# Two transformer blocks on one core: weights ahead of tables, small copies between units, and sums, groups and last units in another order

## The chip, the core and the metric

The kernel runs on one core of a Trainium2 chip. A core has five engines that run side by side: TensorE (PE in the profile) multiplies matrices into PSUM, VectorE (DVE) and ScalarE (ACT) work elementwise, GpSimd (POOL) does so too but reads and writes SBUF only here, and SyncE (SP) issues transfers. Sixteen DMA engines move data between HBM and SBUF. Engines meet through semaphores only, and each works through its own instructions strictly in order. The metric is the time of one execution on the device in microseconds (us); smaller is better.

## What is computed

Two transformer blocks, one after the other, on 256 tokens of 1024 columns, all in float32. The first block has two layers: a mixer of three attentions, a cross-attention to a memory of 256 tokens, and a gated feed-forward (FFN). The second block takes a context of 256 tokens as well. Its shifts, scales and gates come from two vectors times a large matrix `ada_w` (adaLN).

```python
for l in range(DEPTH):                                   # first block, DEPTH = 2
    h = rmsnorm(x, g_mix_pre[l])
    ... = jnp.split(h @ w_in[l], IN_SPLITS, axis=-1)     # three attentions on the parts
    x = x + rmsnorm(concatenate([o_a, o_b, o_c]) @ w_out[l], g_mix_post[l])
    xo = cross_attention(rmsnorm(x, g_x_pre[l]), rmsnorm(mem, g_x_mem[l]), w_xq[l], w_xkv[l], w_xo[l])
    x = x + rmsnorm(xo, g_x_post[l])
    gate, up = jnp.split(rmsnorm(x, g_ffn_pre[l]) @ w_ffn_in[l], 2, axis=-1)
    x = x + rmsnorm((jax.nn.silu(gate) * up) @ w_ffn_out[l], g_ffn_post[l])
for i in range(DEPTH):                                   # second block
    m = (s_c @ ada_w[i] + ada_b[i]); mc = (s_cc @ ada_w[i] + ada_b[i])
    x = half_step_ffn(x, m[:, 0], m[:, 1], m[:, 2], ffn_w_in[i, 0], ffn_w_out[i, 0], ...)
    ...                                                  # context too (i = 0), then
    ...                                                  # neighbourhood attention (i = 0) or convolution (i = 1)
    x = half_step_ffn(x, m[:, 6], m[:, 7], m[:, 8], ffn_w_in[i, 1], ffn_w_out[i, 1], ...)
```

## The kernel before

**The stream of weights.** All weights are laid out as 654 units of up to 128 x 1024 numbers, and every unit goes the same way. SP loads it into `land`, a ring of four slots. ACT rounds it into `w_hi` (`split`, L892). POOL writes the rest, `land` minus `w_hi`, into `w_lo` in two halves (`lo`, L787). PE multiplies twice 2 tiles of tokens with it, three products for each (hi by hi, lo by hi, hi by lo: L2138 to L2140), so a unit costs PE 12 matmuls. SP may load unit u once POOL has done unit u-4 (semaphore `lo_ready`), ACT may split it once PE has done u-4 (`w_used`), and PE waits for `lo_ready` of the unit itself. The first four units' `w_lo` are made by DVE.

**By unit or by tile.** `group` takes four units one after the other with both token tiles (12 matmuls to a unit). `group_by_tile` takes the four units for token tile 0 (6 matmuls each), then again for tile 1; only the second pass gives the units free. `first_group` uses the latter. Its `aside` form, in the FFN that takes x into the second block and in the first product of the neighbourhood attention (`products`, weights `na_w_kv`), puts its results in the PSUM banks `TURN` and `OUT` so that it need not wait for banks 0 to 3, in which the norm before it is still worked on.

**The opening.** `make_h(now=True)` turns x into h: PE transposes it, DVE scales it, ACT writes `h_hi` (`high`), DVE `h_lo`. In this ACT also splits units 0 to 3 and, in `load_constants`, issues nine transfers: eight tables (semaphore `start_in`) and the memory (`io`). In `products_in` (weights `w_in`, groups g = 0 to 3 of four units, so units 0 to 15) ACT's `tables` squares the memory, waits for the eight tables and for DVE's angles (`start_v`), and computes exponentials, cosines and sines. After it stand the next splits. `turn_mem` transposes the memory after group 1. `kv_weights` follows: seven copies of `na_rpb`, each of 1024 rows of 64 numbers from HBM to HBM (`rpb_w`), then the 16 units of `w_xkv`, used in `mixer_prep` and in the mixer's attention.

**The adaLN sums.** `ada_w` comes in 36 groups of four pieces, loaded by SP between the units (`ada_begin`, `ada_finish`), each piece once DVE has done with the same piece of the group before. DVE multiplies and adds a group (`ada_sums`, L2048 and L2051; 16 steps in groups 0 to 9, where both vectors count, 8 later), PE adds over partitions (`ada_sum`, L2739 and L2740), and DVE adds the bias (`ada_rows_out`, L2071). Only then may the next group be summed. Where the sums stand is written by hand: one in each turn of an `ffn_in` loop, one in `products_q`, one or two in `products_y` for `w_xo`, and some in `ffn_out` after the units named in `ADA_OUTS`.

**The end of an FFN.** `ffn_out` has 22 units; k counts them. The last four go to token tile 0 first, its left half of columns over the four units, then its right half, each half ending with `y_ready`. Tile 1 follows. Where `then` is given, PE transposes the next input before the last four (`make_h`), and `turn_free` there waits for the last sum to be out (`ada_sum`).

**Before the neighbourhood attention** SP has `load_tables` asked: after four units of the next weights it loads a mask, a table and 24 quarters of biases (`load_bias`, L723), and then the next unit.

## Time and profile before

| | us |
|---|---|
| median of 3 runs (2251.19 to 2258.12) | 2252.46 |
| the profiled execution, by the same clock | 2254.71 |
| its span from the first to the last instruction | 2252.8 |
| PE busy (matmul) | 2154.2, 96% of the span |
| POOL busy | 1686.8, 75% |
| ACT busy | 1070.5, 48% |
| DVE busy | 966.1, 43% |

All later times are microseconds from the span's start. A row of the timeline gives an instruction's start and length, and in brackets how long its engine was idle before it and who released it. Busy time of PE is modelled for pipelined matmuls, so it is read for gaps, not for peak rate. [...]

### The profile page before, as it was taken

Reading aid. Unit: us, or ns where it says so; the run is one execution under the profiler, and the core shown is the slowest. Engines: PE = TensorE matmul, PEld = TensorE weight load, DVE = VectorE, ACT = ScalarE, POOL = GpSimd, SP = SyncE. Lnnn points to the kernel's source line nnn. Section 1 sums busy time; section 2 is a strip of 40 time slices with the busy share of each in tenths; the row PEclk is TensorE's granted clock in tenths of the full one; section 3 lists DMA queues with packets and bytes.
Section 4 is the critical chain, followed back from the end, with each engine's and each line's share of the span. In section 5 each row is a group of like instructions: output and inputs, shape, how many; then the busy total and the mean of one; then the engine's idle time right before and its main releaser. Section 6 shows DMA issues by size and latency. Waiting matters only on the chain.

```text
span 2252.8 us, 32261 instructions
## 1 busy us (share of the span) xinstructions
PE 2154.2 (96%) x10197; PEld 1741.4 (77%) x10197; DVE 966.1 (43%) x1892; ACT 1070.5 (48%) x1646; POOL 1686.8 (75%) x1361
## 2 busy tenths in 40 slices
PE   8998899999988999999999999999999999999997
PEld 6787778778877787788778877887887788687886
DVE  6355676753556544544543552364111310344112
ACT  4464444445653544444454454565444544435442
POOL 5646388877544888798888879726988888697986
PEclk9999999999999999999999999999999999999999
DMA  7535387755244786687878765523656566464663
GB/s 232 165 113 163 103 296 257 261 182 166 92 138 179 260 284 255 211 300 244 296 255 284 282 218 162 187 76 113 203 179 198 166 186 207 139 222 145 193 205 120
DMA packets 135863, 447.10 MB, mean 198 GB/s; under 512 B 22539, under 2 KB 28131, under 8 KB 135769
## 3 DMA queue, kind: packets, MB, share of 16 engines
q1 hardware_dynamic: 129080, 426.62, 57.4%
q10 hardware_dynamic: 6688, 19.23, 2.5%
q8 instruction: 58, 0.95, 0.2%
q14 instruction: 37, 0.30, 0.0%
HBM read 444.60 MB, written 3.03 MB: 199 GB/s over the span
## 4 chain that ended last, share of the span: by engine, by line
POOL 49%; issue 29%; PE 20%; DVE 1%; POOLq 1%; ACT 0%; DMA 0%; SPq 0%; ACTq 0%; DVEq 0%
POOL w_lo L787 48%; PE ps L2138 5%; PE ps L2140 5%; PE ps L2139 5%; PE ps L2647 1%; PE ps L2612 1%; PE ps L2635 1%; PE ps L2475 1%; POOLq L187 0%; PE ps L2608 0%; POOL ada_land L833 0%; POOLq L785 0%; PE ps L2578 0%; PE ps L2390 0%; PE ps L2580 0%
## 5 line engine op out<-in xcount | busy, mean ns | idle before, releaser
L787 POOL TENSOR_TENSOR w_lo<-land,w_hi 128x512 fp32r<-128x512 f32 x1300 | 1650.3, 1303 | 518.0 <-ACT w_hi L892 516.9
L892 ACT ACTIVATE w_hi<-land 128x1024 fp32r<-128x1024 f32 x654 | 692.5, 1061 | 942.4 <-PE ps L2140 736.9
L2138 PE MATMUL ps<-w_hi,h_hi 128*128 128x512 f32 (+1 forms) x1840 | 734.6, 399 | 52.8 <-POOL w_lo L787 24.4
L2140 PE MATMUL ps<-w_hi,h_lo 128*128 128x512 f32 (+1 forms) x1840 | 720.6, 392 | 0.0
L2139 PE MATMUL ps<-w_lo,h_hi 128*128 128x512 f32 (+1 forms) x1840 | 719.5, 391 | 0.0
L2138 PEld LDWEIGHTS ps<-w_hi,h_hi 128*128 128x128 f32 x1840 | 348.0, 189 | 150.1 <-POOL w_lo L787 39.6
L2140 PEld LDWEIGHTS ps<-w_hi,h_lo 128*128 128x128 f32 x1840 | 347.8, 189 | 74.0
L2139 PEld LDWEIGHTS ps<-w_lo,h_hi 128*128 128x128 f32 x1840 | 348.4, 189 | 67.3
L1530 DVE TENSOR_TENSOR hid_lo<-ps,hid_hi 128x512 f32 (+1 forms) x77 | 53.2, 691 | 550.5 <-ACT hid_hi L1044 550.5
L2138 PE MATMUL ps<-w_hi,hid_hi 128*128 128x512 f32 x616 | 245.2, 398 | 5.7 <-POOL w_lo L787 5.7
L2140 PE MATMUL ps<-w_hi,hid_lo 128*128 128x512 f32 x616 | 243.5, 395 | 0.0
L2139 PE MATMUL ps<-w_lo,hid_hi 128*128 128x512 f32 x616 | 243.4, 395 | 0.0
L2051 DVE SCALAR_TENSOR_TENSOR ps<-ada_land,ccol,ps 128x512 f32<-128x512 f32 x322 | 230.5, 750 | 20.6 <-DMA ada_land<-ada_w_dram 12.6
L2138 PEld LDWEIGHTS ps<-w_hi,hid_hi 128*128 128x128 f32 x616 | 115.7, 188 | 36.5 <-POOL w_lo L787 7.9
L2140 PEld LDWEIGHTS ps<-w_hi,hid_lo 128*128 128x128 f32 x616 | 115.7, 188 | 28.0
L2139 PEld LDWEIGHTS ps<-w_lo,hid_hi 128*128 128x128 f32 x616 | 115.8, 188 | 27.0
L1128 ACT ACTIVATE h_hi<-ps 128x512 fp32r<-128x512 f32 x56 | 33.0, 597 | 61.6 <-DVE ps L1479 33.1
L2138 PE MATMUL ps<-w_hi,m_hi 128*128 128x512 f32 x128 | 53.6, 418 | 5.1 <-POOL w_lo L787 3.6
L1647 DVE TENSOR_TENSOR hid<-ps,sg 128x256 f32<-128x256 f32 x110 | 41.1, 415 | 37.8 <-ACT sg L1038 37.8
L1727 DVE SCALAR_TENSOR_TENSOR ps<-ps,rows 128x512 f32<-128x512 f32 x24 | 15.9, 693 | 93.2 <-PE ps L2140 93.2
L2140 PE MATMUL ps<-w_hi,m_lo 128*128 128x512 f32 x128 | 51.2, 400 | 0.0
L2139 PE MATMUL ps<-w_lo,m_hi 128*128 128x512 f32 x128 | 51.2, 400 | 0.0
(276 smaller groups left out, 1911.4 us busy)
## 6 DMA issues: line engine op xcount, KB each, us to landing
land<-ffn_w_in_dram SPq DMA_DIRECT2D x220, 512.0 KB, 3.6
ada_land<-ada_w_dram SPq DMA_DIRECT2D x144, 512.0 KB, 5.2
land<-ffn_w_out_dram SPq DMA_DIRECT2D x110, 512.0 KB, 4.1
land<-w_ffn_in_dram SPq DMA_DIRECT2D x88, 512.0 KB, 3.9
land<-w_ffn_out_dram SPq DMA_DIRECT2D x44, 512.0 KB, 4.1
land<-na_w_qkv_dram SPq DMA_DIRECT2D x40, 512.0 KB, 4.2
land<-w_xkv_dram SPq DMA_DIRECT2D x32, 512.0 KB, 3.6
land<-w_in_dram SPq DMA_DIRECT2D x32, 488.0 KB, 3.5
```

The costliest lines, as they stand in the source:

```text
L787: done = pool.tensor_tensor(w_lo[:, slot, half], land[:, slot, half], w_hi[:, slot, half].bitcast(F32), ALU.subtract)
L892: act.activation(w_hi[:, slot, :], land[:, slot, :], ACT.Copy).then_inc(*my.up("hi_ready"))
L1128: act.activation(half_of(h_hi, i), turned_bank(i), ACT.Copy).then_inc(*my.up("split_hi"))
L1530: dve.tensor_tensor(lo_dst, bank(TURN + kp).rearrange("p (a b) -> p a b", a=2), hi_src.bitcast(F32), ALU.subtract).then_inc(*my.up("split_ ...
L1647: ins_ = dve.tensor_tensor(hid[:, g % 2, t, :], got, sg[:, t, :], ALU.mult)
L2051: ins_ = dve.scalar_tensor_tensor(acc, w, c, acc, ALU.mult, ALU.add)
L2138: pe.matmul(dst, lh, wh, start=first, stop=False)
L2139: pe.matmul(dst, lh, wl, start=False, stop=False)
L2140: done = pe.matmul(dst, ll, wh, start=False, stop=last)
L2475: done = pe.transpose(ps[0:m, b, c * SEQ + t * P:c * SEQ + (t + 1) * P], tile, ident[:, :])
L2612: yield pe.matmul(s[:, t * SEQ:(t + 1) * SEQ], q[:, t * P:(t + 1) * P], k, start=(c == 0), stop=(c == len(mp["qk"]) - 1))
L2635: done = pe.transpose(ps[:, TURN + m % 2, at * P:(at + 1) * P], e[:, j * P:(j + 1) * P], ident[:, :])
```

## The change

Five things, none of which changes what is computed.

1. **Opening.** The eight small tables are issued by SP, after unit 3, and not by ACT. ACT writes the first piece of `h_hi` ahead of its first split, and issues only the memory, after the last piece of `h_hi`. `tables` is cut in two: the squares of the memory come after the split of unit 7, the rest after that of unit 8 (both came after unit 6).
2. **Small copies.** The seven copies of `na_rpb` are issued one by one behind units 7 to 13 of the 16 of `w_xkv`, no longer ahead of them.
3. **adaLN sums.** In `products_q` the first result is moved out between the two halves of the sum's steps. In `products_y` PE's sum stands after the fourth unit's first pass, not the third; where two groups are loaded, the second starts at unit 5, not 3, and its last pieces all follow unit 7. In `ffn_out` the sums move from units 7, 12, 17 to 8, 13, 17 (layer 0 of the first block), from 7, 13 to 8, 13 (layer 1), and from 7, 12, 17 to 8, 12, 16 (the two FFN halves that open the second block); SP starts loading each three units ahead, not two.
4. **First group aside.** It goes unit by unit.
5. **Last four units.** Tile 0 takes both halves of units 0 and 1, then the left half of 2 and 3, then their right halves.

```diff
-ADA_OUTS, ADA_OUTS_2, COLUMNS_AT = (7, 12, 17), (7, 13), 9
+ADA_OUTS, ADA_OUTS_2, ADA_OUTS_3, COLUMNS_AT = (8, 13, 17), (8, 13), (8, 12, 16), 9
...
+LAST_FOUR = ((0, 0), (0, 1), (1, 0), (1, 1), (2, 0), (3, 0), (2, 1), (3, 1))
...
+            def products_in(l):
+                stream(f"w_in{l}", 0, 16, None if l else {RING - 1: load_constants})
...
             def kv_weights(w):
                 if n_kv[0] == 0:
-                    for j in range(7):
...
-                stream(w, 0, KV_UNITS)
+                    stream(w, 0, KV_UNITS, {RPB_AT + j: lambda j=j: shifted_rpb(j) for j in range(7)}, rolled=False)
+                else:
+                    stream(w, 0, KV_UNITS)
...
-                extra = ada_extra([3] if keys else [0, 3][0:sums])
+                extra = ada_extra([3] if keys else [0, 5][0:sums])
+                if sums > 1:
+                    late = [extra.pop(at) for at in (8, 9)]
+                    extra[7] = lambda steps=[extra[7], *late]: [step() for step in steps]
...
-                extra = ada_extra([at - 2 for at in ada])
+                extra = ada_extra([at - 3 for at in ada])
...
                 if l == 0:
+                    split(RING)
+                    square_memory()
+                    split(1)
+                    tables()
                     split(RING - 1)
-                    tables()
-                    split(RING + 1)
...
                 if now:
+                    high(0)
                     split(1)
-                    high(0)
                     high(1)
                     split(RING - 1)
-                    load_constants()
                     high(2)
                     high(3)
+                    load_io("mem")
                     return
...
             def products_q(w):
                 dve.wait_ge(*my.last())
-                ada_sums()
+                ada_steps(range(0, KC // 2))
                 scaled_out("q_x", 0, GW, 0, R_X, "taken")
-                dve.wait_ge(*my.last())
+                ada_sums(range(KC // 2, KC))
                 ada_rows_out()
...
             def first_group(width, aside):
 
-                group_by_tile((TURN, OUT) if aside else (0, 2), width, fresh=True, aside=aside)
-                if aside:
+                if not aside:
+                    group_by_tile((0, 2), width, fresh=True)
+                else:
+                    pe.wait_ge(sems["split_lo"], my.at("split_lo", n["split_lo"]))
+                    group((TURN, OUT), width)
...
                 if sums:
-                    after[2] = ada_sum
+                    after[3] = ada_sum
...
-                for half in range(2):
-                    for j in range(4):
-                        if half == 0:
-                            pe.wait_ge(sems["lo_ready"], my.at("lo_ready", u + j + 1))
-                        done = part(u + j, FC - 4 + j, {0: (half,)})
-                    done.then_inc(*my.up("y_ready"))
+                for j, half in LAST_FOUR:
+                    if half == 0:
+                        pe.wait_ge(sems["lo_ready"], my.at("lo_ready", u + j + 1))
+                    done = part(u + j, FC - 4 + j, {0: (half,)})
+                    if j == 3:
+                        done.then_inc(*my.up("y_ready"))
```

In what order the instructions now stand is shown at three places. ACT at the opening, before: the end of `load_constants`, the last two pieces of `h_hi`, the squares of x, three splits, then all of `tables`.

```order
L909 DMA ghead<-diff_head_g_dram 128x128
L909 DMA io<-mem_dram 128x2x1024
L1128 ACTIVATE h_hi<-ps 128x4x128 x2
L1095 ACTIVATE z,stat<-x 128x1024 x2
L1079 DMA rows<-g_mix_post_dram 128x1024
L1082 DMA vals<-mla_w_q_up_dram 128x2x384
L1083 DMA vals<-mla_w_kv_up_dram 128x512
L892 ACTIVATE w_hi<-land 128x1024 x3
L927 ACTIVATE z,stat<-io 128x1024 x2
L929 ACTIVATE csig<-ccol 128x16
L931 ACTIVATE lam<-lam 128x4
L932 ACT_TABLE_LOAD
```

The same stretch of ACT in the changed kernel, from the splits of units 1 to 3 on.

```order
L920 ACTIVATE w_hi<-land 128x1024 x3
L1144 ACTIVATE h_hi<-ps 128x4x128 x2
L1102 DMA io<-mem_dram 128x2x1024
L1111 ACTIVATE z,stat<-x 128x1024 x2
L1095 DMA rows<-g_mix_post_dram 128x1024
L1098 DMA vals<-mla_w_q_up_dram 128x2x384
L1099 DMA vals<-mla_w_kv_up_dram 128x512
L920 ACTIVATE w_hi<-land 128x1024 x4
L939 ACTIVATE z,stat<-io 128x1024 x2
L920 ACTIVATE w_hi<-land 128x1024
L943 ACTIVATE csig<-ccol 128x16
L945 ACTIVATE lam<-lam 128x4
```

The two pieces of `h_hi` no longer stand behind transfers, and two more splits stand ahead of the exponentials. DVE in `products_q` (layer 0), before: 16 steps of a sum (L2048, L2051), its rounding, and then the first result (`tok_x`).

```order
L2048 TENSOR_SCALAR ps<-ada_land,ccol 128x512 x2
L2051 SCALAR_TENSOR_TENSOR ps<-ada_land,ccol,ps 128x512 x14
L2057 CAST ada_hi<-ps 128x512 x2
L2060 TENSOR_TENSOR ada_lo<-ps,ada_hi 128x512 x2
L1556 TENSOR_SCALAR tok_x<-ps,stat 128x512 x2
L2071 TENSOR_TENSOR ada_o<-ps,ada_b 2x512
```

And in the changed kernel:

```order
L2063 TENSOR_SCALAR ps<-ada_land,ccol 128x512 x2
L2066 SCALAR_TENSOR_TENSOR ps<-ada_land,ccol,ps 128x512 x6
L1572 TENSOR_SCALAR tok_x<-ps,stat 128x512 x2
L2066 SCALAR_TENSOR_TENSOR ps<-ada_land,ccol,ps 128x512 x8
L2078 CAST ada_hi<-ps 128x512 x2
L2081 TENSOR_TENSOR ada_lo<-ps,ada_hi 128x512 x2
L2092 TENSOR_TENSOR ada_o<-ps,ada_b 2x512
```

The first result went ahead of half the steps and of the rounding. SP at `products_y` of `w_xo` in layer 1, before, from the third unit on: the piece of `ada_land` that belongs to the second group stands, with the one before it (x2), ahead of the fifth unit.

```order
L621 DMA land<-w_xo_dram 128x1024
L576 DMA ada_land<-ada_w_dram 128x1024
L621 DMA land<-w_xo_dram 128x1024
L576 DMA ada_land<-ada_w_dram 128x1024 x2
L621 DMA land<-w_xo_dram 128x1024
L589 DMA ada_m<-ada_o 2x512
L594 DMA ada_b<-ada_b_dram 1x512
L576 DMA ada_land<-ada_w_dram 128x1024
L621 DMA land<-w_xo_dram 128x1024
```

And in the changed kernel:

```order
L625 DMA land<-w_xo_dram 128x1024
L580 DMA ada_land<-ada_w_dram 128x1024
L625 DMA land<-w_xo_dram 128x1024
L580 DMA ada_land<-ada_w_dram 128x1024
L625 DMA land<-w_xo_dram 128x1024
L593 DMA ada_m<-ada_o 2x512
L598 DMA ada_b<-ada_b_dram 1x512
L625 DMA land<-w_xo_dram 128x1024
L580 DMA ada_land<-ada_w_dram 128x1024
L625 DMA land<-w_xo_dram 128x1024
```

The fifth and sixth units now stand ahead of every piece of the second group.

## Rows read from the trace of the kernel before

**Rows 1.** Page: busy (share) xinstructions; POOL's `w_lo` (xcount, busy, mean ns, idle, releaser)

```profile
PE 2154.2 (96%) x10197; PEld 1741.4 (77%) x10197; DVE 966.1 (43%) x1892; ACT 1070.5 (48%) x1646; POOL 1686.8 (75%) x1361
...
L787 POOL TENSOR_TENSOR w_lo<-land,w_hi 128x512 fp32r<-128x512 f32 x1300 | 1650.3, 1303 | 518.0 <-ACT w_hi L892 516.9
```

**Rows 2.** PE's waits over the span: us in total, times, longest

```profile
PE ps L2138 <- POOL w_lo L787: 33.7, 37, 4.6
```

**Rows 3.** Stretches: length; busy (x) of PE, PEld, DVE, ACT, POOL; PEclk, DMA, GB/s

```profile
37.00:44.00 7.00, 6.01 (x17) 5.00 (x18) 6.79 (x8) 1.87 (x3) 6.95 (x6) 0.52 0.49 143
...
71.00:75.00 4.00, 4.00 (x11) 3.13 (x12) 3.62 (x18) 2.54 (x4) 4.00 (x4) 0.57 0.53 153
225.00:232.00 7.00, 4.83 (x16) 4.20 (x17) 2.12 (x4) 1.46 (x3) 3.61 (x3) 0.51 0.53 214
...
45.20:66.74 21.54, 21.54 (x99) 18.13 (x98) 9.05 (x25) 6.92 (x12) 13.91 (x11) 1.00 0.90 232
```

**Rows 4.** Timeline of ACT in the opening: start, us, what, [idle before, releaser]

```profile
18.18 0.60 ACT L1128 ACTIVATE h_hi<-ps 128x512 fp32r<-128x512 f32 x1 [5.29 <-issue]
...
27.58 1.06 ACT L927 ACTIVATE z<-io 128x1024 f32<-128x1024 f32 x1 [2.55 <-DMA io<-mem_dram]
...
32.55 0.20 ACT L931 ACTIVATE lam<-lam 128x4 f32<-128x4 f32 x1 [2.67 <-DVE lam L1437]
...
34.32 3.88 ACT L892 ACTIVATE w_hi<-land 128x1024 fp32r<-128x1024 f32 x4
```

**Rows 5.** Timeline of PE in the opening: units 0, 7 and 16

```profile
19.65 0.46 PE L2138 MATMUL ps<-w_hi,h_hi 128*128 128x488 f32 x1 [0.61 <-DVE h_lo L1488]
...
37.99 0.78 PE L2138 MATMUL ps<-w_hi,h_hi 128*128 128x488 f32 x1 [4.65 <-POOL w_lo L787]
...
70.94 0.50 PE L2138 MATMUL ps<-w_hi,m_hi 128*128 128x512 f32 x1 [3.60 <-POOL w_lo L787]
```

**Rows 6.** Timeline of SP's queue: the seven small copies

```profile
49.67 7.87 SPq L671 DMA_DIRECT2D rpb_w<-na_rpb_dram  x7
```

**Rows 7.** Timeline of PE and DVE in `products_q`, layer 0

```profile
227.17 1.97 PE L2475 MATMUL ps<-ident,tok_x 128*128 128x128 f32 x8 [4.93 <-DVE tok_x L1556]
...
213.85 9.31 DVE L2051 SCALAR_TENSOR_TENSOR ps<-ada_land,ccol,ps 128x512 f32<-128x512 f32 x14
```

**Rows 8.** Timeline of SP, DVE and PE at `w_xo`, layer 1

```profile
681.25 30.48 SPq L576 DMA_DIRECT2D ada_land<-ada_w_dram  x2
...
726.65 0.69 DVE L2060 TENSOR_TENSOR ada_lo<-ps,ada_hi 128x512 fp32r<-128x512 f32 x1
...
729.24 0.50 PE L2138 MATMUL ps<-w_hi,h_hi 128*128 128x512 f32 x1 [0.41 <-POOL w_lo L787]
```

**Rows 9.** Timeline of PE and DVE at `w_xo`, layer 0

```profile
270.38 0.39 PE L2739 MATMUL ps<-ada_hi,pick_r 128*2 128x512 f32 x1 [2.52 <-DVE ada_lo L2060]
...
276.53 1.28 DVE L1698 SCALAR_TENSOR_TENSOR x<-ps,stat,x 128x1024 f32<-128x1024 f32 x1
```

**Rows 10.** Timeline of PE at sums inside `ffn_out`: layer 0, layer 1, second block

```profile
437.09 0.40 PE L2739 MATMUL ps<-ada_hi,pick_r 128*2 128x512 f32 x1 [1.22 <-DVE ada_lo L2060]
...
892.55 0.39 PE L2739 MATMUL ps<-ada_hi,pick_r 128*2 128x512 f32 x1 [1.08 <-DVE ada_lo L2060]
...
1118.21 1.94 PE L2506 MATMUL ps<-ident,x 128*128 128x128 f32 x16 [1.07 <-DVE ada_o L2071]
```

**Rows 11.** Timeline of PE and ACT at the first group aside, in `ffn_in`

```profile
1133.98 0.50 PE L2138 MATMUL ps<-w_hi,h_hi 128*128 128x512 f32 x1 [1.24 <-POOL w_lo L787]
...
1138.95 1.21 ACT L1209 ACTIVATE z<-ps,stat 128x1024 f32<-128x1024 f32 x1
```

**Rows 12.** Timeline of SP and PE at the first group aside, weights `na_w_kv`

```profile
1319.20 15.88 SPq L723 DMA_DIRECT2D ada_land<-rpb_w  x24
...
1343.40 0.47 PE L2138 MATMUL ps<-w_hi,h_hi 128*128 128x512 f32 x1 [0.28 <-POOL w_lo L787]
```

**Rows 13.** Timeline of PE in the last FFN: the last of its 22 units

```profile
2232.09 0.50 PE L2138 MATMUL ps<-w_hi,hid_hi 128*128 128x512 f32 x1 [1.69 <-POOL w_lo L787]
```

61 lines of the change are left out of this document (33 added, 28 removed).

## The prediction

> **What bounds the kernel now.** I read the page first, then the list of waits, then the timeline of each place that the diff touches. PE is busy for 96% of the span. POOL, next in line, works 2 x 1.303 = 2.61 us on a unit of weights and still idles 518 us waiting for ACT, whose splits wait for PE to free the ring [rows 1]. PE itself takes 2.69 us for a unit: 8 units in the 21.54 us of a stretch without any wait [rows 3]. So PE is the bound, by a margin of 3% over POOL, and a time is gained only where PE stands still or runs at its lower clock, and only if no other chain is next in line there. Standing still for POOL's `w_lo` sums up to 33.7 us in 37 waits [rows 2]. After a long stop the granted clock is at about half: 0.52 in 37 to 44, 0.57 in 71 to 75, 0.51 in 225 to 232 [rows 3]; each follows a stop of 3.6 to 4.9 us [rows 5, 7]. A removed stop therefore gives back more than its own length.
>
> **The opening.** Three things go. (a) ACT writes the third piece of `h_hi` after 5.29 us in which it only issued transfers, and PE then waits 0.61 us for `h_lo` [rows 4, 5]; now the pieces are ready first. With the first piece ahead of the first split DVE starts about 0.4 us sooner. I take 1.0 together. (b) ACT splits unit 7 at 34.32, behind `tables`: it waited 2.55 us for the memory and 2.67 us for DVE's angles, and PE stood 4.65 us [rows 4, 5]. The splits of units 7 and 8 now stand ahead. (c) That stop was followed by the lower clock. PE ended unit 7 at 43.0, 5.0 us after its start instead of 2.7: 2.3 us.
> What is late next? POOL needs the split of unit 8 at about 31. ACT has unit 7 split at about 25, the squares take 2.1 us, so the memory may land as late as 28; it is issued some 3 us earlier than before, when it had landed by 27.58 [rows 4]. DVE can start the angles at about 21, after the norm of x, instead of 25, so they end near 28, the memory's norm at 30.5 and the first result at 32; PE wants that at 34.4. The distances (6 us before, beside POOL) and the second result end near 44, and PE wants them at 47. All hold with 2 to 3 us to spare. PE's path then is its own pace.
> (d) The seven copies took SP 7.87 us to issue, ahead of unit 16, and PE stood 3.60 us for that unit [rows 6, 5]; the unit itself then took 4.3 us at half clock instead of 2.7 [rows 3]. Together 5.2. The copies' new place costs nothing: one is 1.1 us of issue, and behind it a unit of weights is asked for about three units ahead of its use, 8 us at PE's full pace and more in the mixer's attention. If this cover were gone, a unit would be late by a copy's stay on the DMA engines.
> Sum of the opening: 1.0 + 4.65 + 2.3 + 5.2 = 13.2 us.
>
> [...] The rows say that the eight tables cost ACT its issue time, 5.29 us, of which PE saw 0.61 [rows 4, 5]. [...]
>
> **The sum in `products_q`, layer 0.** PE stands 4.93 us for `tok_x`, which DVE writes only after 16 steps (14 of them take 9.31) and the rounding [rows 7]. Now 8 steps, 5.3 us, stand ahead of it, so it is out at 219.3 and PE, there at 222.2, does not stop. The lower clock after the stop cost 2.1 us more (8 transposes and 12 matmuls). In exchange the sum is ready only at 227.1 (8 steps 5.3, rounding 2.6), where PE arrives at 225.9: a new wait of 1.2. Net 5.8. Layer 1 has sums of 8 steps and no such stop: 0.
>
> **The sums at `w_xo`.** In layer 0 PE waits 2.52 us for DVE [rows 9]; one pass of a unit later, 1.4 us less. But behind it PE needs the new x, which DVE ends at 277.8 [rows 9] at the end of a chain that starts from the same sum. Of 1.4 only 0.2 arrive. In layer 1 SP held the fifth unit behind a piece of the second group for 30 us [rows 8], and PE ran through five waits, the last at 729.24. Now two more units are there early, and the second group is DVE's: it ends at 727.34 [rows 8], PE's second pass can begin at 728.3 instead of 730.6, and DVE's chain to x gives back 1.4 of these 2.3. Take 1.4.
>
> **The sums in `ffn_out`.** Layer 1: the wait of 1.08 goes, with what its first matmul shows around it 1.2. Second block, both halves: the wait of 1.07 for `ada_o` [rows 10] is covered by one more unit: 1.2 for the first; the second is dealt with below. Layer 0 is different: a sum there takes DVE 15.1 us (437.09 [rows 10] to the next at 452.2), and 13 to 17 are four units, 11.2 us. The first wait of 1.22 goes, but the third sum comes 3 x 15.1 us after DVE's start plus the 1.4 us that DVE now waits for PE at unit 8. PE stands 2.7 us at unit 17 and passes it 1.3 us later than before. The 0.63 us wait in its last four units goes with that. Net a loss of 0.5.
>
> **The first group aside.** By tile, PE takes 1.35 us for a unit that POOL needs 2.6 for, so the first pass has waits of 1.24, 0.82 and 0.81 (the first is in [rows 11]); by unit it has none. In `ffn_in` ACT cannot split the next unit before it has normalised, at 1138.95 + 1.21 [rows 11], so PE, done sooner, waits for it: of 3.9 us I keep 2.2. Before the neighbourhood attention nothing is kept. There the next unit is not asked for before SP has issued 24 biases, 15.88 us, until 1335.1; it reaches PE at 1343.40 [rows 12]. The waits removed (the sum's 1.2, the passes' 2.9) come back as one stop of about 6 us before that same unit. Stops of 3.6 to 4.9 us were followed by half clock three times out of three [rows 3]. One unit then takes 5 us instead of 2.7, two can be hit; and DVE copies x beside POOL earlier. Bounds: -4.5 and +0.5 (nothing lost, the ring fuller). I take -2.5.
>
> [...]
>
> **The last four units.** The last of the 22 units is ready 1.69 us after PE wants it [rows 13], in three FFNs (also at 1732.77 and 1931.51). Now PE has two more parts of 0.70 us to do first: 1.4 each. In the last FFN DVE's chain starts at the end of the first left half, which the same `w_lo` sets, and is busy from there to the end: only 0.5. First `y_ready` comes 1.4 us later against the second, which hides a scaling of 0.7. Sum 3.3.
>
> **Total.** 13.2 + 5.8 + 0.2 + 1.4 + 1.2 + 1.2 - 0.5 + 2.2 - 2.5 + 3.3 = 25.5 us. Against the profiled execution, 2254.7 with a span of 2252.8, this gives 2229.2; the median of the runs lies 2.2 lower, 2252.5, so I forecast 2227.0.
>
> **Rivals.**
> - *Half clock stays away before the neighbourhood attention, and chains give more back.* For it: 2 us stops are often not followed by the lower clock. Then -2.5 becomes 0, and layer 0 or `w_xo` may give 2 more: 2222.5.
> - *The opening is held by another chain.* DVE's distances run beside POOL, and if they or the memory end 3 to 5 us later than I count, PE stops again and half clock follows (2 us): 7 us lost, 2234.
> - *The gain stays off the path, POOL being the bound.* The chain of waits goes through POOL for half of the span, and POOL's pace is only 3% under PE's. Then only stops in which POOL idled too are worth something, the opening's 13.2 and little else: 2239. Against it: POOL's 518 idle us end with ACT, whose waits end with PE [rows 1].
> - *Slower: the small copies starve the mixer.* The seven copies lie between units 7 and 14 on SP's queue. If each holds the unit behind it past PE's need, by its stay on the DMA engines (7 copies and a unit kept the DMA full for some 11 us, 1.6 each), and PE comes back at half clock each time (2.3), that is 7 x 3.9 = 27 us and cancels the rest: 2254; with stops of over 1.8 us the kernel is slower. It decides when a unit is asked for less than 5 us ahead; it is asked for over 8.
> - *The change does not do what it says*: ACT would have to reach `tables` before unit 7 all the same. The order shown rules it out.
>
> **Chances.** Forecast 0.60, better case 0.16, opening held 0.14, POOL as bound 0.06, copies 0.03, the rest 0.01. The forecast's own bounds are 2222 to 2232, from the -4.5 to +0.5 and some 2 us for where the clock's changes fall. With the rivals on both sides but the last ones: 2219 to 2237. About 0.3% (6.8 us) is what a measurement of this kernel can tell from no change: faster 0.95, same 0.03, slower 0.02.
>
> **What would show it.** Right: no wait over 1 us of PE for `w_lo` before 60 us, the first matmul of unit 16 near 58; no stop for `tok_x`, and a wait of about 1.2 for `ada_lo` behind it; a stop of 2 to 3 us for `ada_lo` at unit 17 of layer 0's `ffn_out`; a stop of 5 to 6 us for `w_lo` near 1310 with a clock near 0.5 behind it; 0.3 instead of 1.69 at the last units. Wrong: PE waiting for `zin` or the memory in the opening, ACT waiting for `w_xkv` to land in the mixer, or PE's busy time at full clock growing.

## The result, and the profile after

The kernel after takes 2226.45 us (median of 4 runs, 2223.64 to 2231.67), the kernel before 2255.29 beside it (4 runs, 2251.19 to 2261.65). The ratio is 0.987, 95% interval 0.984 to 0.991. The forecast was 2227.0, with bounds of its own from 2222 to 2232, and 2219 to 2237 with the rivals on both sides, so the time came out as forecast. The profiled execution of after took 2223.64 us, 5.4 and 8.0 less than the upper two of the four runs: that gap is the part of the story the forecast did not have.

The page of after answers [rows 1]: PE is busy 13.1 us less, with the same 10197 multiplications, and POOL idles 29 us less.

```profile
PE 2141.1 (96%) x10197; PEld 1735.5 (78%) x10197; DVE 968.2 (44%) x1892; ACT 1069.0 (48%) x1646; POOL 1684.8 (76%) x1361
...
L815 POOL TENSOR_TENSOR w_lo<-land,w_hi 128x512 fp32r<-128x512 f32 x1300 | 1648.4, 1300 | 489.4 <-ACT w_hi L920 488.0
```

PE's list of waits over the span (us in total, times, longest) answers [rows 2]. Waits for `w_lo` fell from 33.7 us in 37 to 18.6 in 22, but the longest grew from 4.6 to 7.4; waits for the adaLN sums, 6.1 us in 4 before, stand in the second row.

```profile
PE ps L2159 <- POOL w_lo L815: 18.6, 22, 7.4
PE ps L2763 <- DVE ada_lo L2081: 9.1, 5, 2.8
```

Both kernels issue PE's multiplications in nearly the same order, so the n-th of before can be set against the n-th of after. The difference of their starts, in the two profiled executions, grows where after gains. Each row below is read between two places at which it stands still; the last row takes the difference of the two spans. PEclk is TensorE's granted clock as a share of full speed. Half clock is a stretch in which it read 0.50, as from 38 to 44 us of before; a figure between 0.50 and 1.00 is the mean of a stretch with both.

| place | difference at the end of it, us | gained there | forecast |
|---|---|---|---|
| opening: units 0 to 3 | 1.9 | 1.9 | 1.0 |
| opening: units 7 and 8 | 9.5 | 7.6 | 6.95 |
| opening: unit 16 | 14.9 | 5.4 | 5.2 |
| `products_q`, layer 0 | 20.7 | 5.8 | 5.8 |
| `w_xo`, layer 0 | 21.65 | 1.0 | 0.2 |
| sums in `ffn_out`, layer 0 | 21.1 | -0.5 | -0.5 |
| half clock that only before had (484, 624 us), and cross-attention of layer 1 | 23.05 | 1.9 | none |
| `w_xo`, layer 1 | 24.8 | 1.7 | 1.4 |
| sums in `ffn_out`, layer 1 | 26.0 | 1.2 | 1.2 |
| second block, first half | 27.2 | 1.3 | 1.2 |
| first group aside, `ffn_in` | 29.6 | 2.3 | 2.2 |
| before the neighbourhood attention | 27.6 | -2.0 | -2.5 |
| last four units | 31.0 | 3.4 | 3.3 |

The timeline of PE in after at the places of [rows 5, 7, 10, 12, 13] (start, length, what, in brackets the idle time before and its releaser). Unit 7 and unit 16 follow the work ahead of them without a stop: they have no bracket.

```profile
31.35 0.38 PE L2159 MATMUL ps<-w_hi,h_hi 128*128 128x488 f32 x1
...
57.60 0.48 PE L2159 MATMUL ps<-w_hi,m_hi 128*128 128x512 f32 x1
...
212.31 0.40 PE L2763 MATMUL ps<-ada_hi,pick_r 128*2 128x512 f32 x1 [1.30 <-DVE ada_lo L2081]
...
447.06 0.40 PE L2763 MATMUL ps<-ada_hi,pick_r 128*2 128x512 f32 x1 [2.81 <-DVE ada_lo L2081]
...
1316.19 0.77 PE L2159 MATMUL ps<-w_hi,h_hi 128*128 128x512 f32 x1 [7.42 <-POOL w_lo L815]
...
2201.72 0.50 PE L2159 MATMUL ps<-w_hi,hid_hi 128*128 128x512 f32 x1 [0.34 <-POOL w_lo L815]
```

The third row is the small wait that `products_q` was to get in exchange (forecast 1.2, read 1.30), the fourth the one at unit 17 of layer 0's `ffn_out` (forecast 2.7, read 2.81), the fifth the long stop (forecast about 6, read 7.42), the last the remainder at the last units (forecast 0.3, read 0.34). The stretches around the old and the new stop (length; busy time of PE, PEld, DVE, ACT, POOL; PEclk; DMA; GB/s) answer [rows 3]: full clock where before had half, and half where the new long stop is.

```profile
37.00:44.00 7.00, 7.00 (x33) 5.94 (x32) 6.86 (x7) 4.27 (x9) 6.96 (x6) 1.00 0.67 210
1312.00:1319.00 7.00, 2.81 (x7) 2.26 (x8) 4.11 (x3) 3.66 (x4) 6.44 (x5) 0.53 0.60 209
```

### The profile page after: what moved, and what is told of

The parts are those of the page before. It is cut to its first block, busy times and chain, and to the rows that moved or that the text cites. A ratio compares the mean times of both kernels' runs of the same rounds, so it can differ in the third digit from the quotient of the medians.

```text
span 2221.8 us, 32201 instructions
## 1 busy us (share of the span) xinstructions
PE 2141.1 (96%) x10197; PEld 1735.5 (78%) x10197; DVE 968.2 (44%) x1892; ACT 1069.0 (48%) x1646; POOL 1684.8 (76%) x1361
## 4 chain that ended last, share of the span: by engine, by line
POOL 49%; issue 27%; PE 21%; DVE 2%; POOLq 1%; DMA 0%; ACT 0%; SPq 0%; ACTq 0%; DVEq 0%
POOL w_lo L815 48%; PE ps L2159 6%; PE ps L2161 6%; PE ps L2160 6%; PE ps L2671 1%; PE ps L2636 1%; PE ps L2659 1%; PE ps L2499 1%; POOLq L191 0%; PE ps L2632 0%; POOL ada_land L861 0%; POOLq L813 0%; PE ps L2602 0%; PE ps L2414 0%; DMA cols<-cols_dram 0%
```

## The experiments

Every kernel below is the kernel after with the edit shown. The difference of starts is now taken against after's profiled execution, at the place of the edit, since whole runs of one kernel lie up to 0.4% apart.

### The order of ACT's splits

```diff
                 if l == 0:
-                    split(RING)
+                    split(RING - 1)
                     square_memory()
-                    split(1)
                     tables()
-                    split(RING - 1)
+                    split(RING + 1)
```

> The kernel after, but ACT does the squares of the memory and all of tables behind the split of unit 6 again, as before; the eight tables stay on SP's queue. If the order of ACT's splits is what took the stop of unit 7 away (the prediction's step b), a stop comes back there, of the length that the later of two ends dictates: the memory lands in time now, DVE's angles end at 28.6, the sines at 30.5, the split of unit 7 at 31.5, and PE wants the unit at 31.35: a stop of 1 to 2 us, without half clock, 14.9 us of gain by unit 16 become 13 to 14. If the earlier landing had nothing to do with it (only order counts), the whole stop of about 5 us and its half clock return: the gain is about 8. If the order counts for nothing, no stop and no loss.

One run took 2229.70 us. PE in it, at unit 7:

```profile
34.03 0.49 PE L2158 MATMUL ps<-w_hi,h_hi 128*128 128x488 f32 x1 [2.63 <-POOL w_lo L815]
```

The stop is back with 2.8 us lost and no half clock behind it. So both halves count: the order takes 2.8 us away. The rest of the 7.6 us that were gained at units 7 and 8 remains in this kernel, in which ACT began the squares of the memory at 23.49 with no wait, where [rows 4] had 27.58. That the earlier issue of the tables and the memory gives this rest is got by subtraction, not by a run of its own. The stop is longer than the 1 to 2 us that I expected, because I counted to the end of the split: POOL's two halves, 2.6 us, stand between it and PE.

### Who issues the tables

```diff
-                stream(f"w_in{l}", 0, 16, None if l else {RING - 1: load_constants})
+                stream(f"w_in{l}", 0, 16, None)
...
                     split(RING - 1)
+                    load_constants()
                     high(2)
```

> The kernel after, but ACT issues the eight tables itself, behind the split of unit 3 and ahead of the third piece of h_hi; all else stays. By the prediction's step a this is worth ACT's issue time as far as PE saw it: a wait for h_lo of 0.6 to 1 us returns and the gain by unit 16 falls from 14.9 to about 14, with no stop for unit 7 or 8. The rival, that the tables held ACT and DVE through their later landing: DVE's angles start some 5 us later, its distances and second result go past 47 us, and PE stops for these by 3 us or more between units 8 and 16: a gain of 11 or less.

One run took 2233.61 us. DVE's `h_lo`, the first of its operations on the positions, and PE's transposes of the memory in it:

```profile
16.93 1.29 DVE L1520 TENSOR_TENSOR h_lo<-ps,h_hi 128x512 fp32r<-128x512 f32 x2 [1.71 <-ACT h_hi L1159]
...
23.70 1.01 DVE L1454 CAST pos_r<-pos_i 128x256 f32<-128x256 int32 x1 [1.58 <-DMA ghead<-diff_head_g_dram]
...
38.74 3.06 PE L2526 MATMUL ps<-ident,io 128*128 128x128 f32 x16 [4.40 <-DVE zin L1588]
```

6.4 us are lost by unit 9, and the rival is the one that describes it: the tables held DVE through their landing (positions at 23.70 instead of 19.00), and DVE's first result (`zin`) held PE. The wait for `h_lo`, by which the prediction priced ACT's issue time, did not come back: `h_lo` starts at 16.93 where before had 18.82, and PE keeps level with after, within 0.2 us, up to 30 us. The 6.4 are measured against an execution of after in which PE had no stop for `zin`. Six others with after's opening had one and were 4.4 to 4.8 us later than it by unit 9 (below); against those, the tables on ACT's queue cost 1.5 to 2.0. ACT's issue time, 5.29 us in before, of which PE saw 0.61, was the wrong measure for them: the queue's issue stands ahead of the landing of the last table (`diff_head_g`, issued at 14.98 us here and at 7.80 in after), and what waits for that is a chain on another engine.

### The seven small copies

```diff
-                    stream(w, 0, KV_UNITS, {RPB_AT + j: lambda j=j: shifted_rpb(j) for j in range(7)}, rolled=False)
+                    for j in range(7):
+                        shifted_rpb(j)
+                    stream(w, 0, KV_UNITS)
```

> The kernel after, with the seven copies ahead of unit 16 again. Theory (step d): PE stops for unit 16 by about 3.6 us and works it at half clock, 5.2 us in all, and the copies' new place had cost nothing, so the gain falls by 5.2 and by nothing else. Rival: the ring is fuller at this place than it was before, so that the 7.9 us of issue are hidden in part: a loss under 2 us.

One run took 2230.24 us. SP's issue of the copies, and PE at unit 16:

```profile
41.90 8.30 SPq L691 DMA_DIRECT2D rpb_w<-na_rpb_dram  x7
...
61.87 0.50 PE L2161 MATMUL ps<-w_hi,m_hi 128*128 128x512 f32 x1 [3.73 <-POOL w_lo L817]
```

5.6 us are lost there (0.3 to 5.9 behind after), forecast 5.2. From there to 440 us the difference stays within 0.25; later it moves between 5.5 and 8.3, mostly with half clock that falls at other places in the two executions. The copies' new place cost nothing: against before, after's gain stays at 14.9 from 76 to 200 us.

### `products_q` in its old order

```diff
-                ada_steps(range(0, KC // 2))
+                ada_sums()
                 scaled_out("q_x", 0, GW, 0, R_X, "taken")
-                ada_sums(range(KC // 2, KC))
+                dve.wait_ge(*my.last())
                 ada_rows_out()
```

> The kernel after, with products_q in its old order: all steps of the sum and its rounding ahead of the first result. Theory: PE stops 4.9 us for tok_x in layer 0, half clock costs 2.1 behind it, and the wait of about 1.2 for the sum goes: a loss of 5.8, and nothing in layer 1. Rival: the loss is made good further on, at the wait for x behind w_xo, whose chain starts from a sum: then less than 3 us are left by the end of layer 0.

One run took 2240.85 us. PE, and the stretch around it with a granted clock of 0.58:

```profile
217.96 1.97 PE L2499 MATMUL ps<-ident,tok_x 128*128 128x128 f32 x8 [4.98 <-DVE tok_x L1572]
...
214.00:221.00 7.00, 3.04 (x11) 2.76 (x12) 3.87 (x6) 2.25 (x3) 5.34 (x5) 0.58 0.82 322
```

The difference goes from 5.6 to 11.1: 5.5 us, forecast 5.8. Up to the last sum of layer 0, at 447 us of after, it stays at 11.1, so nothing was made good. Most of the rest of this run's length lies in the opening (4.6) and in half clock near 1461 us (3.2), both below.

### The sums of layer 0

```diff
-ADA_OUTS, ADA_OUTS_2, ADA_OUTS_3, COLUMNS_AT = (8, 13, 17), (8, 13), (8, 12, 16), 9
+ADA_OUTS, ADA_OUTS_2, ADA_OUTS_3, COLUMNS_AT = (7, 12, 17), (8, 13), (8, 12, 16), 9
```

> The kernel after, with the sums of layer 0's ffn_out back at units 7, 12 and 17 (SP still three units ahead). The prediction put the new places there at a loss of 0.5 us, its argument being that DVE's 15.1 us for a sum don't fit between 13 and 17. Theory: by the end of this FFN 0.5 us are won, the wait at the first sum, 3.2 us in the kernel after, becoming one of 1.2 at the first and one or two smaller. Rival: the gap at 443.9 comes from DVE's late start and is there whatever the places are; no difference.

One run took 2236.84 us, and yet the place itself gains: the difference falls from 5.4 to 4.0 over the three sums, 1.4 us. The first sum waits 1.23 us, the third not at all:

```profile
420.87 0.39 PE L2763 MATMUL ps<-ada_hi,pick_r 128*2 128x512 f32 x1 [1.23 <-DVE ada_lo L2081]
```

The forecast of -0.5 for the edit holds against before (21.65 to 21.1). The undone edit gains more than that: the two things the edit did together, later places and an earlier start of SP's loading, are then worth -1.4 and, by subtraction, +0.9. `result_first` below, which has the same places, gains the same 1.4. I had expected 0.5, or nothing.

### The long stop: by tile, and with PE kept busy

```diff
...
-                first_group(width, aside)
+                if aside:
+                    group_by_tile((TURN, OUT), width, fresh=True, aside=True)
+                    for t in range(T):
+                        name, value = free[t]
+                        pe.wait_ge(sems[name], my.at(name, value))
+                else:
+                    first_group(width, aside)
                 group((1, 3), width)
```

> The kernel after, with the first group aside of the neighbourhood attention by tile again; that of ffn_in stays by unit. The prediction put this part at -2.5 us there together with a gain of 1.2 from the sum ahead of it. Theory: three waits of 0.8 to 1.2 us return, the one stop of 7.8 shrinks to 4 to 5, and half clock stays or goes by that: a gain of 0 to 2.5 us against the kernel after. Rival: the unit behind the biases comes at the same time whatever stands ahead, so nothing changes within 0.5 us.

One run took 2237.25 us. At the place, three waits are back (the first is shown) and the long one shrinks to 2.20:

```profile
1308.89 0.50 PE L2159 MATMUL ps<-w_hi,h_hi 128*128 128x512 f32 x1 [1.25 <-POOL w_lo L815]
...
1323.13 0.47 PE L2159 MATMUL ps<-w_hi,h_hi 128*128 128x512 f32 x1 [2.20 <-POOL w_lo L815]
...
1320.00:1327.00 7.00, 4.38 (x19) 3.03 (x18) 5.86 (x5) 3.89 (x5) 6.51 (x5) 1.00 0.63 221
```

The clock stays full (the last row), and the difference goes from 8.6 to 7.3: by tile was better here by 1.35 us. To part the half clock from the stop, the next kernel fills it:

```diff
                 first_group(width, aside)
+                if aside:
+                    hold(1, 8)
                 group((1, 3), width)
```

> The kernel after, with eight multiplications of no use (0.85 us each, into bank 1, which the next group overwrites) in the stop of 7.8 us before the second group of the neighbourhood attention. The stop itself stays as long, since it ends with w_lo. If the half clock of 1312 to 1319 us comes from the stop, it goes, and with it 2 to 3 us; the loss of the first group aside there falls from 8.6 (7.8 and what stands around it) to about 6. If the clock fell for another reason, it stays and nothing changes, or the held PE starts the group later, by up to 1 us.

One run took 2230.82 us. `hold` runs until 1322.46, PE then waits 0.73 more for the unit, and the stretch behind it is at full clock, where after had 0.77 in the matching one:

```profile
1315.43 7.03 PE L2167 MATMUL ps<-dist,ident 128*128 128x512 f32 x16
1323.18 0.50 PE L2159 MATMUL ps<-w_hi,h_hi 128*128 128x512 f32 x1 [0.73 <-POOL w_lo L815]
...
1323.00:1330.00 7.00, 6.82 (x30) 5.64 (x31) 0.00 (x0) 2.54 (x3) 7.00 (x7) 1.00 0.52 166
```

So the half clock comes from the stop. The other profiled executions agree: the nine of after's kind whose stop here was 4.4 us or longer had half clock at it, the three whose stop was 2.2 or less had none. It is worth 1.2 us (6.8 to 5.6), not 2 to 3: half of the 7 us at half clock lay in the stop itself, and what PE lost in the next unit it had in part from waits for POOL that were there anyway. The rest of the loss is the stop.

### The biases spread

```diff
-                stream("na_w_qkv" if w == "na_w_kv" else w, first, 4 * groups)
+                if w == "na_w_kv":
+                    stream("na_w_qkv", first, 4 * groups, {RING + 1 + 2 * h: lambda h=h: load_bias(h) for h in range(NA_BIAS - 1)} | {4 * groups - 1: lambda: load_bias(NA_BIAS - 1)}, rolled=False)
+                else:
+                    stream(w, first, 4 * groups)
...
                 sp.dma_start(ada_land[:, 1, T * SEQ:T * SEQ + 128], ins["na_rope"]).then_inc(sems["na_in"], 16)
-                for h in range(NA_BIAS):
-                    load_bias(h)
```

> The kernel after, with the 24 transfers of biases not in one piece ahead of the second group of the neighbourhood attention, but four behind every second unit of na_w_kv. Theory (the stop of 7.8 us is SP's 15.8 us of issue ahead of the next unit): the stop and the half clock go, unless DVE's or ACT's work on x is next in line: 7 to 9 us faster than the kernel after. Rival: ACT's split of the next unit waits for the norm of x as in ffn_in, so a stop of 3 to 4 us stays, without half clock: 4 to 6 us faster. Against it all: each set of four holds the unit behind it, four stops of 1 us or more: no gain.

Four runs, median 2224.35 us (2220.69 to 2227.04), ratio to before 0.987, 0.984 to 0.990. SP now issues four quarters, then two units, in turn, and PE's longest wait at the place is 1.41:

```profile
1306.63 2.54 SPq L754 DMA_DIRECT2D ada_land<-rpb_w  x4
1309.22 2.38 SPq L625 DMA_DIRECT2D land<-na_w_qkv_dram  x2
1311.64 2.37 SPq L754 DMA_DIRECT2D ada_land<-rpb_w  x4
...
1316.16 0.47 PE L2160 MATMUL ps<-w_hi,h_hi 128*128 128x512 f32 x1 [1.41 <-POOL w_lo L816]
...
1311.26 1.21 ACT L1226 ACTIVATE z<-ps,stat 128x1024 f32<-128x1024 f32 x1
1312.37 2.94 ACT L921 ACTIVATE w_hi<-land 128x1024 fp32r<-128x1024 f32 x3
```

The difference goes from 6.0 to 0.25, so 5.8 us are won at the place: the rival's 4 to 6, for its reason, though its stop of 3 to 4 us is three waits of 2.3 together. The last two rows show it: ACT writes the norm of x first and splits the next units behind it, as in `ffn_in`. 1.6 us of the gain are lost again near 1450 us, below.

### The late edits undone

```diff
-ADA_OUTS, ADA_OUTS_2, ADA_OUTS_3, COLUMNS_AT = (8, 13, 17), (8, 13), (8, 12, 16), 9
+ADA_OUTS, ADA_OUTS_2, ADA_OUTS_3, COLUMNS_AT = (8, 13, 17), (7, 13), (7, 12, 17), 9
-LAST_FOUR = ((0, 0), (0, 1), (1, 0), (1, 1), (2, 0), (3, 0), (2, 1), (3, 1))
+LAST_FOUR = ((0, 0), (1, 0), (2, 0), (3, 0), (0, 1), (1, 1), (2, 1), (3, 1))
```

> The kernel after, with three late edits undone at places that can be read apart: the sums of layer 1's ffn_out at 7 and 13, those of the second block's two opening halves at 7, 12 and 17, and the last four units by whole half columns. Theory, term by term: 1.2 us lost at the first sum of layer 1; 1.2 in the first half of the second block; in its second half the 1.2 are lost ahead of the first group aside and given back at the stop of 7.8 us; and in the last four units 1.4 lost in two FFNs and 0.5 in the last. Rival (POOL is the bound, so what PE loses here was waiting behind it anyway): each of these places loses under 0.5 us.

One run took 2231.57 us. Lost against after: 0.9 at layer 1's sums, 1.27 in the second block's first half, 1.27 in its second half ahead of the aside group, and 1.36, 1.36 and 0.6 in the three FFNs whose last unit PE waits for. That is theory's list, and the rival with POOL as the bound falls. The 0.9 is the weakest of them: kernels without this edit lost 0.2 to 1.1 at the same place against after, which has no wait there. PE in the second half, and at the stop behind it:

```profile
1292.07 1.94 PE L2530 MATMUL ps<-ident,z 128*128 128x128 f32 x16 [1.07 <-DVE ada_o L2092]
...
1320.71 0.77 PE L2159 MATMUL ps<-w_hi,h_hi 128*128 128x512 f32 x1 [4.36 <-POOL w_lo L815]
```

But the stop gives back 2.9 us, more than the 1.27. The rest points at SP's queue. Its waits in after, in the 27 us ahead of the biases, hold one that the same stretch of before does not have (the first row); with the sum back at unit 17 it is 2.7 (the second row, of `late_undo`):

```profile
SPq L593 <- DVE ada_o L2092: 3.8, 1, 3.8
...
SPq L593 <- DVE ada_o L2092: 2.7, 1, 2.7
```

SP stores a sum's result once the next sum's pieces are through. In before that store stood behind unit 19 of this FFN's 22, the edits (a sum earlier by one unit, loading a unit earlier too) put it behind unit 17, and SP stood there 3.8 us for a result that was not yet out. It reached the biases 6.6 us after PE's transposes began (1291.15 against 1284.53 on PE) where before and this kernel had 3.9 (1319.20 against 1315.33, 1295.93 against 1292.07). Of these 2.75 us, 1.25 are PE's own lead, the wait for the sum that is gone, and 1.5 are SP's delay. Without that delay the stop would have been near the forecast 6. The delay came with the sum's new place: eleven more profiled executions that have it show 0.8 to 1.9 us of it, `late_undo` none. But `late_undo` too had 2.7 us of the wait, so that the longer wait for the store makes the delay is argued, and not shown apart from the rest of the edit.

### Why the executions of after fall in two groups

Six kernels whose opening is that of after had, in their profiled execution, a stop which after's lacks. This is `bias_spread`:

```profile
37.21 2.79 PE L2511 MATMUL ps<-ident,io 128*128 128x128 f32 x16 [3.27 <-DVE zin L1573]
```

| profiled execution | DVE begins the angles (`ang`) | POOL begins | ahead by | PE's granted clock 10 to 16 us | PE waits for `zin` | PE by unit 9, later than after |
|---|---|---|---|---|---|---|
| `after` | 19.54 | 20.58 | 1.04 | 0.72 | 0 | 0 |
| `after_again` | 19.44 | 20.38 | 0.94 | 0.72 | 0 | -0.25 |
| `copies_ahead` | 19.71 | 20.87 | 1.16 | 0.72 | 0 | +0.3 |
| `clock_hold` | 19.80 | 19.99 | 0.19 | 1.00 | 3.27 | +4.5 |
| `aside_by_tile` | 20.05 | 20.25 | 0.20 | 1.00 | 3.20 | +4.7 |
| `q_undo` | 19.92 | 20.14 | 0.22 | 1.00 | 3.24 | +4.6 |
| `sums_layer0` | 19.81 | 19.98 | 0.17 | 1.00 | 3.27 | +4.4 |
| `late_undo` | 19.71 | 19.89 | 0.18 | 1.00 | 3.24 | +4.4 |
| `bias_spread` | 20.19 | 20.38 | 0.19 | 1.00 | 3.27 | +4.8 |

DVE's angles are a dozen small operations, each waiting for the last. The same one of them, first in after, then in `bias_spread`, and the start of POOL in each (rows in this order):

```profile
20.07 0.18 DVE L1443 TENSOR_SCALAR ang<-ang 128x32 f32<-128x32 f32 x1
...
21.75 1.22 DVE L1444 TENSOR_SCALAR ang<-ang 128x32 f32<-128x32 f32 x1
...
20.58 29.95 POOL L815 TENSOR_TENSOR w_lo<-land,w_hi 128x512 fp32r<-128x512 f32 x23 [19.60 <-ACT w_hi L920]
...
20.38 12.65 POOL L816 TENSOR_TENSOR w_lo<-land,w_hi 128x512 fp32r<-128x512 f32 x10 [19.40 <-ACT w_hi L921]
```

In after it took 0.18 us, before POOL had begun; in `bias_spread` 1.22, with POOL at work: about one half of a `w_lo` (1.27). Not all of DVE's small operations are slowed. Beside the same POOL, those of 128 x 2 numbers with an operand in PSUM take 0.17 (the first row, of after), and so does one of 128 x 1 in SBUF (the second). Then come the first result in `bias_spread` and in after:

```profile
29.31 0.17 DVE L1401 SCALAR_TENSOR_TENSOR ps<-ps,newton 128x2 f32<-128x2 f32 x1
...
33.34 0.15 DVE L1472 TENSOR_SCALAR lam<-lam 128x1 f32<-128x1 f32 x1
...
35.80 1.36 DVE L1573 TENSOR_SCALAR zin<-ps,stat 128x488 f32<-128x488 f32 x2
...
30.91 1.36 DVE L1572 TENSOR_SCALAR zin<-ps,stat 128x488 f32<-128x488 f32 x2
```

So a lead of 1.0 us over POOL instead of 0.2 lets several operations through at 0.2 instead of 1.2 each, and the first result starts at 30.91 instead of 35.80 (the last two rows). PE wants it at about 34.0. The rows show which steps POOL slowed: 1.2 us for a step of the angles, 128 x 32 numbers in SBUF, and no delay for the steps of 128 x 2 numbers with an operand in PSUM (0.17). By what mechanism, no run shows, and why the step of 128 x 1 was spared (0.15) stays open.

What gives the lead is a turn that nobody would plan: where PE had half clock over units 0 and 1 (0.72 in 10 to 16 us), it gave unit 0 free later, ACT split unit 4 later, and POOL began later against DVE. Half clock at 12 us cost 0.8 us and saved the stop and the half clock behind it, 5.1 in all. That this is so in nine of nine profiled executions, and in `tables_back` as a tenth (0.72, ahead by 1.02, no wait for `zin`), shows the order of events. The half clock itself goes with the arrival of x: PE begins to transpose x at 6.25 to 6.55 us in the seven executions of this kind that had it, `tables_on_act` and the two of the next section among them, and at 6.62 to 6.73 in the six that had not. Why stays open. Whether all of the spread between executions has this cause was asked of the kernel itself:

> The kernel after, unchanged. The profiles of five kernels with the same opening show PE waiting 3.3 us for DVE's first result (zin) and then half clock, 4.9 us in all, where the profiled execution of the kernel after had none of it. If this is a race between DVE's angles and POOL's first w_lo, decided by when x lands, the executions of this kernel lie in two groups some 5 us apart, about 2223 and 2229, with the median near 2227. If it was an accident of those kernels, they lie together near 2224.

Four runs: 2222.60, 2227.65, 2228.47 and 2230.76 us, median 2228.06, ratio to before 0.989 (0.987 to 0.991). With the four shown at the top, three of eight executions lie at 2222.6 to 2223.9 and five at 2227.7 to 2231.7. The profiled one, 2222.60, is of the lower group and has no stop. No execution of the upper group was profiled for this kernel, so that its cause is the stop rests on the times and on the six other kernels. The groups are 6.1 us apart on average, the stop makes 4.4 to 4.8 of it.

### The first result ahead of the rest of the angles

```diff
                     step(dve.scalar_tensor_tensor(ang[:, 0, :, :], ang[:, 3, :, :], -piece, ang[:, 0, :, :], ALU.mult, ALU.add))
+
+            def angles_end():
                 step(dve.tensor_scalar(ang[:, 1, :, :], ang[:, 0, :, :], PI_IN, -PI_IN, ALU.min, ALU.max))
...
                 scaled_out("zin", 0, IN_GW, 0, R_X, "taken")
                 if l == 0:
+                    angles_end()
+                scaled_out("zin", 1, IN_GW, 1, R_X, "taken")
+                if l == 0:
                     tables()
                     distances()
-                scaled_out("zin", 1, IN_GW, 1, R_X, "taken")
...
                     square_memory()
-                    split(1)
-                    tables()
                     split(RING - 1)
+                    tables()
+                    split(1)
```

First with the biases spread and layer 0's sums put back, then alone.

> The kernel after with three edits: the biases spread, the sums of layer 0's ffn_out back at 7, 12, 17, and in the opening DVE writes its first and second result ahead of the last three operations on the angles and of distances, while ACT splits units 8 to 10 ahead of the exponentials. Theory: DVE's small operations take 1.2 us each beside POOL and 0.2 without it, and the first result stood behind them; now it is out at 29 to 32.4 us, PE wants it at 33.6, and the stop of 3.3 us and its half clock go in every execution: 4.9 us of the opening, with 6 from the biases and 1 from the sums, so 2216 to 2219, 1.5% less than before's 2252. Rival: DVE's chain is only moved, and its later results (m_lo, the rotated keys, the third result) stop PE further on by 3 us or more: 2220 to 2224.

Four runs: 2218.24, 2220.02, 2222.68 and 2224.66 us, median 2221.35, ratio to before 0.985 (0.983 to 0.987). It is 6.7 below the median of after's four runs of the same chip. That misses theory's 2216 to 2219 and lies where the rival put it, but not for the rival's reason: nothing later than the opening waits for DVE's postponed work, and up to 400 us the difference to after is 0.15 or less. In the profiled execution 3.2 us were lost near 1450, at half clock (below).

> The kernel after with the opening's edit alone: DVE writes its first and second result ahead of the last three operations on the angles and of distances, ACT splits units 8 to 10 ahead of the exponentials. Of eight executions of the kernel after three took 2222.6 to 2223.9 us and five 2227.7 to 2231.7. Theory (the upper group is the one in which DVE's angles run beside POOL and PE stops for zin): with this edit the upper group is gone, the executions lie between 2221 and 2226 with the median near 2223.5, and the profile shows PE waiting under 0.5 us for zin whichever way the angles fell. Rival (the groups come from half clock elsewhere, at 450, 600 or 700 us): the two groups stay, median near 2227.

Four runs: 2222.14, 2222.54, 2222.98 and 2226.99 us, median 2222.76, ratio to before 0.987 (0.984 to 0.989). Three of four lie where three of eight did. The fourth is the profiled one, and its extra length is not in the opening: PE reaches the memory at 34.06 with no wait, as after does, and loses 0.8 us at 217, 1.5 at 450 and 1.6 at 603 and behind it.

```profile
34.06 1.91 PE L2514 MATMUL ps<-ident,io 128*128 128x128 f32 x16
...
27.30 0.16 DVE L1395 TENSOR_SCALAR ps<-stat 128x2 f32<-128x2 f32 x1 [5.28 <-ACT z L939]
29.69 1.36 DVE L1574 TENSOR_SCALAR zin<-ps,stat 128x488 f32<-128x488 f32 x2
```

Both profiled executions with this edit had the lead over POOL, so neither shows the edit at work where the lead is missing. The second row gives an estimate: DVE had 5.28 us to spare ahead of the first result. In `bias_spread`, without the lead, the steps that still stand ahead of it ended at 27.98, and the 2.4 us from 27.30 to 29.69 behind them give a first result at 30.4, ahead of PE's 34.0. That the upper group is gone is likely, but four executions of `result_first_alone`, three of them at or under 2223.0, are all that speaks for it: `result_first` can't be counted, since its other two edits are worth 7 us at their places and would bring an execution with the stop down to the same times.

### Half clock that moves about

Besides the stop of 7.4 us, half clock turns up in some executions at about 450, 605, 710 and 1450 us, in others not, at the same work and behind stops of 1 to 3 us. The dearest is near 1450, in the neighbourhood attention. The same attention, four kernels (the first row is after, then `bias_spread`, `result_first`, `aside_by_tile`; clock in the column behind POOL's):

```profile
1447.00:1461.00 14.00, 14.00 (x118) 12.21 (x119) 8.03 (x21) 8.53 (x21) 4.31 (x4) 1.00 0.27 70
...
1444.00:1458.00 14.00, 12.48 (x91) 10.72 (x92) 8.12 (x19) 8.27 (x20) 5.07 (x4) 0.88 0.25 67
...
1442.00:1456.00 14.00, 14.00 (x90) 12.14 (x92) 6.28 (x16) 6.67 (x16) 4.03 (x4) 0.76 0.17 48
...
1454.00:1468.00 14.00, 14.00 (x66) 11.69 (x64) 3.85 (x10) 4.97 (x13) 3.82 (x4) 0.52 0.16 44
```

It costs 1.6, 3.2 and 6.4 us in these three. All four kernels that had no half clock near 1316, `clock_hold` among them, had it near 1450; of the nine that had it near 1316, two did. In these four, then, a part of what the shorter stop gained was lost again 130 us later. Why is open, and four against nine is a count, not a cause.

## Why the forecast was right, and where it was not

**The terms.** Nine of the twelve terms, forecast and read, agree within 0.5 us (the table at the top), and where an experiment undid an edit it found the same: 5.6 for the copies (forecast 5.2), 5.5 for `products_q` (5.8), 1.27 for each half of the second block (1.2), 3.3 for the last units (3.3). Term by term this holds between two profiled executions, and each undoing is one run. The rule that carried them, that a stop is worth its length, what it hides, and the half clock behind it, held for the opening and for `products_q`.

**The opening, 13.2, was mis-sized in both directions.** In the profiled execution it gave 14.9: step (a) was 1.9 and not 1.0, and steps (b) and (c) gave 7.6 and not 6.95. Of the 1.9, PE's shorter wait for the first unit is 0.5 (2.98 to 2.44), x landing earlier in this execution 0.2, a shift of the early half clock 0.3, and the wait for `h_lo` [rows 5] 0.8; and `tables_on_act` had no such wait either, so the 0.6 that were put down to ACT's issue time are not shown to come from the tables' place. But in six of nine profiled executions with after's opening, and by the times in five of the eight of after itself, DVE's first result stops PE, and the opening gives 10.1 to 10.5. PE waiting for `zin` was one of the prediction's own signs of being wrong. The step that failed is "DVE can start the angles at about 21 ... so they end near 28". Before's trace could not give the durations: its angles ran while POOL stood idle in the very stop that the change takes away. One step of them, and POOL's next start in before:

```profile
30.13 0.18 DVE L1427 TENSOR_SCALAR ang<-ang 128x32 f32<-128x32 f32 x1
...
35.44 13.52 POOL L787 TENSOR_TENSOR w_lo<-land,w_hi 128x512 fp32r<-128x512 f32 x10 [5.37 <-ACT w_hi L892]
```

With the stop gone POOL works beside them, a step costs 1.2 for 0.18, the first result starts at 35.3 to 35.8 and not at 32, and the 2 to 3 us to spare are used up. This comes close to the rival "the opening is held by another chain", which had 0.14: PE does wait for a chain of DVE's beside POOL, but it is the angles ahead of the first result, and not the distances or the memory, which the rival named. The price was nearer 5 than the 7 forecast.

**The total is right in part by balance.** Term by term 25.5 were forecast and 31.0 read between the two profiled executions. Of the 5.5 more, 1.7 are the opening, 0.8 `w_xo` of layer 0, and 1.9 are half clock that only the execution of before had at 484 and 624 us, an accident. Against the median, the stop for `zin` in the slower executions takes this back: 2226.45, or 2228.1 over the eight runs, against 2227.0. The gain itself was 28.8 us beside before's 2255.29 and, with the same kernels run again, 25.1 (2253.19 to 2228.06), where 25.5 were forecast.

**`w_xo` of layer 0, forecast 0.2, gave 1.0.** The chain to x was taken as starting at the same time as before. PE's wait for the sum fell from 2.52 to 1.07, and 1.0 of it reached the units behind.

**Before the neighbourhood attention, -2.5 forecast, -2.0 read,** for a reason that was half right. The stop was 7.42 and not about 6, since SP came to the biases 1.5 us later than its old pace. The prediction said that SP's issue ended it, and took the beginning of that issue from before: the store of a sum's result had been moved two units forward on SP's queue, and waited there 3.8 us. The half clock behind the stop was priced at up to a unit's 2.3 and was 1.2. The two errors cancelled. 5.8 us of stop and half clock were avoidable (`bias_spread`).

**POOL as the bound** (0.06) and **the copies starve the mixer** (0.03) both fell: PE came earlier by the length of each stop that was removed, and POOL idled 29 us less.

## What to carry to other kernels

Give a long run of small transfers to the queue piece by piece between the large ones: 24 quarters in one piece ahead of the next unit of weights cost a stop of 7.4 us, in six lots of four they cost 1.4. Of an edit that moves a step, follow every instruction it issues down to the last store, on each queue: here a store moved two units forward waited 3.8 us, and the loads behind it came 1.5 late. A chain of small operations whose price depends on what a neighbour does at that moment (0.18 us a step here, or 1.2) has no fixed length, and a trace in which the neighbour stood idle gives its best case; keep the result that the bottleneck waits for ahead of it rather than behind it, and profile more than one execution before believing that it fits.

## What the runs showed of the hardware

- DVE's steps on 128 x 32 numbers in SBUF took 0.18 us beside an idle POOL and 1.2 beside a POOL at work; its steps on 128 x 2 numbers with an operand in PSUM took 0.17 in both cases (from 32.62 us of before and from 28.71 us of after).
- Half clock early on went with a faster opening: 0.8 us lost at 12 us saved 5.1 at 34, by the order in which two other engines came to start.
- Filling a stop of 7 us with idle multiplications kept the clock at full (1.00 from 1323 to 1330 us, where after had 0.77 in the matching stretch). It was worth 1.2 us, and half clock came up later at another place.
- Profiled executions of kernels that are alike near 1450 us differed by up to 6.4 us there, by where half clock fell. Eight executions of one kernel lay 0.4% apart, so two single runs that differ by less say nothing; the starts of the same multiplication in two traces, read at the place of the edit, told terms of about 1 us apart.
